# The S5 state scan of a two-block model: tables built in the feed forward before it and kept in DRAM, two groups by 64 states on the partitions, rounds overlapped

## The reference

```
for direction in (0, 1):
    bu_re = jnp.einsum('sgc,gpc->sgp', us, bb_re[direction])
    bu_im = jnp.einsum('sgc,gpc->sgp', us, bb_im[direction])
    ...
    _, _, h_re, h_im = lax.associative_scan(
        _s5_combine, (a_re, a_im, bu_re, bu_im), reverse=(direction == 1), axis=0)
    y = y + (jnp.einsum('sgp,gcp->sgc', h_re, cr[direction])
             - jnp.einsum('sgp,gcp->sgc', h_im, ci[direction]))
y = (y + d_skip.astype(f32) * u).astype(h.dtype)
z = jax.nn.gelu(y)
return (z @ w_glu_a) * jax.nn.sigmoid(z @ w_glu_b)
```

## Time and profile before

| | us |
|---|---|
| median of three runs | 3797.86 (3797.72 to 3806.94) |
| the profiled execution | 3796.62 |
| its span | 3794.7 |
| first feed forward, first matmul to last | 2379.6 to 2838.0 |
| S5, from there to the first matmul of `glu` | 2838.0 to 3209.9 |
| `glu`, second feed forward, end | 3209.9 to 3794.7 |

### The profile page before, as it was taken

How to read it: one execution, slowest core, us unless ns; L and a number is a source line. 1 busy time by engine, 2 the same in 40 slices (tenths; PEclk the granted TensorE clock), 3 DMA queues, 4 the chain that set the end, 5 groups by cost and what they waited for, 6 DMA issues and landing times. The chain is left out here.

```text
span 3794.7 us, 26215 instructions
## 1 busy us (share of the span) xinstructions
PE 3338.5 (88%) x9256; PEld 1562.0 (41%) x9256; DVE 1858.3 (49%) x3813; ACT 726.8 (19%) x1533; POOL 762.4 (20%) x680
## 2 busy tenths in 40 slices
PE   8999799888987888788788999999996777999998
PEld 3444444333433333333333454444444454444443
DVE  5556722676777777776741653115006995110000
ACT  2233211222222222222212111101003222010000
POOL 0110000344444444444420000000002442000000
PEclk9999899999999998988999999999997887999999
DMA  5643312999999999999971310222110000112221
GB/s 190 230 157 119 126 54 77 397 421 421 405 414 422 421 421 421 422 416 414 421 308 61 139 56 33 93 74 77 67 56 23 14 14 25 67 67 78 78 72 73
DMA packets 113540, 743.98 MB, mean 196 GB/s; under 512 B 13136, under 2 KB 13904, under 8 KB 30864
## 3 DMA queue, kind: packets, MB, share of 16 engines
q0 software_dynamic: 88016, 588.82, 38.2%
q1 hardware_dynamic: 25408, 153.67, 11.2%
HBM read 740.34 MB, written 2.10 MB: 196 GB/s over the span
## 5 line engine op out<-in xcount | busy, mean ns | idle before, releaser
L1283 PE MATMUL po<-pair,diag 128*128 128x512 f32 x2048 | 987.1, 640 | 226.4 <-ACT diag L1343 226.2
L1203 POOL DMA_INDIRECT pair<-in_peer_uv,idx x512 | 582.5, 1138 | 960.5 <-PE po L1283 664.1
L1430 DVE SCALAR_TENSOR_TENSOR pair<-pair,h_tm 128x1024 f32<-128x1024 f32 x512 | 617.0, 1225 | 308.1 <-DMA pair<-in_peer_uv,idx 304.4
L1283 PEld LDWEIGHTS po<-pair,diag 128*128 128x128 f32 x2048 | 409.3, 204 | 783.4 <-issue 486.2
L1574 PE MATMUL acc<-a,ring 128*128 128x512 f32 x1024 | 442.9, 593 | 0.0
L1559 PE MATMUL acc<-hT,ring 128*128 128x512 f32 x960 | 412.3, 592 | 0.0
L1574 PEld LDWEIGHTS acc<-a,ring 128*128 128x128 f32 x1024 | 195.1, 191 | 246.1 <-issue 246.1
L1559 PEld LDWEIGHTS acc<-hT,ring 128*128 128x128 f32 x960 | 182.4, 190 | 229.6 <-issue 229.6
L1599 DVE TENSOR_TENSOR a<-a 128x512 f32<-128x512 f32 x64 | 44.4, 693 | 395.0 <-ACT a L1585 395.0
L1606 DVE SCALAR_TENSOR_TENSOR xT<-acc,mod,xT 128x512 f32<-128x512 f32 x16 | 11.9, 750 | 386.9 <-PE acc L1574 386.9
L1337 ACT ACTIVATE ge<-a 128x4 f32<-128x4 f32 x128 | 26.3, 205 | 906.0 <-DVE pair L1430 905.9
(11 more groups left out here) (411 smaller groups left out, 3584.9 us busy)
## 6 DMA issues: line engine op xcount, KB each, us to landing
ring<-in_w_fc SPq DMA_DIRECT2D x62, 1024.0 KB, 4.8
mg<-in_ada_w POOLq DMA_DIRECT2D x96, 512.0 KB, 5.1
ring<-in_w SPq DMA_DIRECT2D x15, 1024.0 KB, 4.8
first<-in_w_first SPq DMA_DIRECT2D x14, 1024.0 KB, 5.7
other<-in_w_first SPq DMA_DIRECT2D x14, 1024.0 KB, 4.9
pair<-in_peer_uv,idx POOLq DMA_INDIRECT x512, 14.8
ring<-in_w_glu SPq DMA_DIRECT2D x7, 1024.0 KB, 4.8
first<-in_w_peer SPq DMA_DIRECT2D x4, 1024.0 KB, 5.4
```

The costliest lines, as they stand in the source:

```text
L1203: pool.indirect_dma_start(out=pair[:, at, :], out_offset=None, in_=core.dram["peer_uv"][:, :], in_offset=bass.IndirectOffsetOnAxis(ap=idx[ ...
L1283: last = pe.matmul(po[:, t % 2, half * 512:(half + 1) * 512], diag[:, at, :], pair[:, at, D + half * 512:D + (half + 1) * 512], start=firs ...
L1430: dve.scalar_tensor_tensor(row, row, 1.0, h_tm[:, t, :], ALU.mult, ALU.mult, accum_out=a[:, g, s:s + 1]).then_inc(dotted, 1)
```

## The change

`s5_tables` takes the place of `s5_powers` as `beside`. It makes the powers in a layout with two groups by 64 states on the partitions (real and imaginary parts now lie side by side in a row, so no swap products exist), and then all round-dependent tables: input weights `tp`, output weights `w2`, cosines, signed sines `turn`, and `decay`. They are 128 x 3328 floats a round (1.7 MB), 16 rounds. VectorE and ScalarE make them between the tiles of the feed forward, GpSimd's queue writes them to DRAM. The stage `s5` replaces the three old stages. SP reads the tables back, four rounds buffered. TensorE works on round i+1's weights while VectorE scans round i, and takes the outputs of round i-1. Products of 64-row halves write different PSUM banks. The rounds are unrolled. The order of the second block's state parameters in DRAM changes with the layout. Core of the diff (`...` marks what is left out):

```diff
         block = st.block()
         if beside:
-            block.gpsimd(load)
+            block.gpsimd(pool)
+        powers_at, rounds_at = [0, 1, 2, 4, 7], [9, 12, 15, 18, 21, 24, 27, 30]
         @block.sync
...
                 act.activation(a[:, n, :], acc[:, n % 3, :], ACT.Relu).then_inc(taken, 1)
+                if beside and n in powers_at:
+                    scalar_powers(act, powers_at.index(n))
+                if beside and n in rounds_at:
+                    scalar_round(act, rounds_at.index(n))
             if beside:
-                scalar(act)
-            act.preload_act_table_set(LN_EXP)
+                scalar_round(act, 8)
             for j in range(KT):
+                if j == KT - 1:
+                    act.preload_act_table_set(LN_EXP)
                 act.wait_ge(added, j + 1)
                 sums.square(act, j)
+                if beside and j < KT - 1:
+                    scalar_round(act, 9 + j)
             sums.root(act)
         @block.vector
...
                 dve.tensor_tensor(a[:, n, :], a[:, n, :], a[:, n, :], ALU.mult).then_inc(squared, 1)
+                if beside and n == 0:
+                    vector_powers(dve)
+                if beside and n in rounds_at:
+                    vector_round(dve, rounds_at.index(n))
             if beside:
-                vector(dve)
+                vector_round(dve, 8)
             for j in range(KT):
                 dve.wait_ge(half_made, 2 * j + 2)
                 x = core.xT[:, j, :]
                 at = gate_col(2 * layer + 1) + j
                 dve.scalar_tensor_tensor(x, acc[:, (N1 + j) % 3, :], core.mod[:, at:at + 1], x, ALU.mult, ALU.add).then_inc(added, 1)
+                if beside and j < KT - 1:
+                    vector_round(dve, 9 + j)
...
+        for r in range(ROUNDS):
+            eng.wait_ge(prepared, r + 1)
+            eng.wait_ge(sined, r + 1)
+            eng.dma_start(core.scratch[r * P:(r + 1) * P, :], table[:, r % 2, :]).then_inc(written[r % 2], 16)
+            if r + 2 < ROUNDS:
+                eng.dma_start(bc[:, r % 2, :], block_of(core, "s5_bc", r + 2)).then_inc(bc_landed[r % 2], 16)
+        for sem in written:
+            eng.wait_ge(sem, 8 * ROUNDS)
...
+    def scalar_round(act, r):
+        if r == 0:
+            act.wait_ge(ready, 5)
+        if r >= 2:
+            act.wait_ge(written[r % 2], 16 * (r // 2))
+        act.wait_ge(tabled, r + 1)
+        turn = piece(r, "turn").rearrange("p (d i q n) -> p d i q n", d=2, i=2, q=2)
+        cos = piece(r, "ct").rearrange("p (g n) -> p g n", n=SN)
+        flat = ang[:, :, :].rearrange("p (d q) n -> p d q n", d=2)
+        act.activation(turn[:, :, 1, :, :], flat, ACT.Sin)
+        act.activation(turn[:, :, 0, :, :], flat, ACT.Sin, scale=-1.0)
+        act.activation(cos, ang[:, :, :], ACT.Abs).then_inc(a_step, 1)
+        act.wait_ge(a_step, r + 1)
+        act.activation(cos, cos, ACT.Sin, scale=-1.0, bias=quarter[:, 0:1]).then_inc(sined, 1)
+    step_of = []
...
+    def vector_round(dve, r):
+        step = step_of[0]
+        here = slice(4 * r, 4 * r + 4)
+        if r >= 1:
+            dve.wait_ge(sined, r)
+        if r >= 2:
+            dve.wait_ge(written[r % 2], 16 * (r // 2))
+        step(dve.tensor_tensor(ang[:, :, :], no[:, :, :], th8[:, here].unsqueeze(2).to_broadcast([P, 4, SN]), ALU.mult))
+        reduced(dve, step, ang[:, :, :], turns[:, :, :], exact=False)
+        dve.tensor_scalar(ang[:, :, :], ang[:, :, :], PI_SAFE, -PI_SAFE, ALU.min, ALU.max).then_inc(tabled, 1)
+        decay = piece(r, "decay").rearrange("p (d i q n) -> p d i q n", d=2, i=2, q=2)
+        rate = r8[:, here].rearrange("p (d q) -> p d q", d=2).unsqueeze(3).to_broadcast([P, 2, 2, SN])
+        for i in range(2):
+            step.mark(dve.tensor_tensor(decay[:, :, i, :, :], keep[:, :, i, :, :], rate, ALU.mult))
+        dve.wait_ge(bc_landed[r % 2], 16 * (r // 2 + 1))
+        b = bc[:, r % 2, 0:128].rearrange("p (i g c) -> p i g c", i=2, g=4)
+        cc = bc[:, r % 2, 128:384].rearrange("p (i g c) -> p i g c", i=2, g=4)[:, :, :, 0:SC]
+        for name, power, with_, first, second in (("tp", pb, b, ALU.add, ALU.subtract), ("w2", pc, cc, ALU.subtract, ALU.add)):
+            out = piece(r, name).rearrange("p (i g t c) -> p i g t c", i=2, g=4, t=ST)
+            for n, (x, i) in enumerate(((0, 0), (1, 1), (1, 0), (0, 1))):
+                step.mark(dve.tensor_tensor(part[:, n, :, :, :], power[:, x, here, :].unsqueeze(3).to_broadcast([P, 4, ST, SC]),
+                                            with_[:, i, :, :].unsqueeze(2).to_broadcast([P, 4, ST, SC]), ALU.mult))
+            step.wait()
+            step.mark(dve.tensor_tensor(out[:, 0, :, :, :], part[:, 0, :, :, :], part[:, 1, :, :, :], first))
+            step(dve.tensor_tensor(out[:, 1, :, :, :], part[:, 2, :, :, :], part[:, 3, :, :, :], second))
+        dve.sem_inc(prepared, 1)
...
+        def _(sp):
+            for i in range(ROUNDS):
+                if i >= 4:
+                    sp.wait_ge(y_done, i - 3)
+                sp.dma_start(tab[:, i % 4, 0:N_TABLE], core.scratch[i * P:(i + 1) * P, :]).then_inc(landed[i % 4], 16)
+                sp.dma_start(tab[:, i % 4, N_TABLE:], block_of(core, "s5_bc", i)[:, 128:384]).then_inc(landed[i % 4], 16)
+                if i == 1:
...
+            def turn(i):
+                pe.wait_ge(landed[i % 4], 32 * (i // 4 + 1))
+                for ri in range(2):
+                    if i >= 1:
+                        pe.wait_ge(w1_copied, 2 * i - 1 + ri)
+                    for g in range(4):
+                        last = pe.transpose(bank[:, ri, g * P:(g + 1) * P], tp(i)[:, ri, g, :], ident[:, :])
+                    last.then_inc(turned, 1)
+            def own(i):
+                if i >= 1:
+                    pe.wait_ge(taps_copied, 2 * i)
+                for d in range(2):
+                    for ri in range(2):
+                        for q in range(2):
+                            for par in range(2):
+                                at = 2 * SP * par // 2 + 32 * q
+                                last = pe.matmul(bank[at:at + 32, 2 + par, d * (ST - 1) * SC:d * (ST - 1) * SC + P],
+                                                 c32(i, half[par])[:, ri, 2 * d + q, :], tp(i, half[par])[:, ri, 2 * d + q, :],
+                                                 start=(d == 0 and ri == 0), stop=(d == 1 and ri == 1), skip_group_check=True)
+                last.then_inc(tapped, 1)
+            def toeplitz(i, part):
+                pe.wait_ge(taps_copied, 2 * i + 2)
+                if part or i:
+                    pe.wait_ge(dm_copied, 2 * i + part)
+                for t in range(4 * part, 4 * part + 4):
+                    at = (ST - 1 - t) * SC
+                    last = pe.transpose(bank[:, 4, (t % 4) * P:(t % 4 + 1) * P], taps[:, i % 2, at:at + P], ident[:, :])
+                last.then_inc(d_made, 1)
+            def ends(i):
+                pe.wait_ge(w1_copied, 2 * i + 2)
+                if i:
+                    pe.wait_ge(framed, i)
+                for q in range(2):
+                    for d in range(2):
+                        for ri in range(2):
+                            at = ((d * 2 + ri) * 2 + q) * SN
+                            for par in range(2):
+                                last = pe.matmul(bank[half[par], 5, at:at + SN], w1[:, i % 2, ri, 2 * d + q, half[par]],
+                                                 u[:, 2 * i + q, half[par]], start=True, stop=True, skip_group_check=True)
+                last.then_inc(ended, 1)
+            def outputs(i):
+                pe.wait_ge(dm_copied, 2 * i + 2)
+                if i:
+                    pe.wait_ge(z_done, 2 * i)
+                for q in range(2):
+                    for par in range(2):
+                        pe.matmul(bank[half[par], 6 + par, q * P:(q + 1) * P], u[:, 2 * i + q, half[par]], dm[:, i % 3, 2 * par + q, :],
+                                  start=(q == 0), stop=False, skip_group_check=True)
+                pe.wait_ge(h_ready, 2 * i + 2)
+                for d in range(2):
+                    for ri in range(2):
+                        for q in range(2):
+                            for par in range(2):
+                                last = pe.matmul(bank[half[par], 6 + par, q * P:(q + 1) * P], hs[half[par], i % 2, d, ri, q, d:d + SN],
+                                                 w2(i, half[par])[:, ri, 2 * d + q, :], start=False, stop=(d == 1 and ri == 1),
+                                                 skip_group_check=True)
+                last.then_inc(y_done, 1)
...
+                    last = pe.transpose(bank[:, 4 + n % 2, g * P:(g + 1) * P], h2[:, 4 * n + g, :], ident[:, :])
+                last.then_inc(u_made, 1)
+            pe.wait_ge(u_copied, 8)
+            toeplitz(0, 0)
+            toeplitz(0, 1)
+            for i in range(ROUNDS):
+                ends(i)
+                if i + 1 < ROUNDS:
```

(40 more changed lines are left out.)

579 lines of the change are left out of this document (211 added, 368 removed).

## The result

The changed kernel takes 3584.89 us (median of four, 3582.02 to 3588.12) against 3798.39 beside it: a ratio of 0.9434, with a 95% interval of 0.9423 to 0.9445. The profiled execution took 3582.96 us.

What follows compares the result with a forecast made beforehand. The prediction took VectorE to set the pace, with table work and a contention in its chain. Feed forward 7.0 us, rounds 148 to 154 and edges the rest summed to -178.5, giving 3619 us; range 3590 to 3700.

Steps and rivals of the forecast that it cites:

- first feed forward: Stage before S5: TensorE's 6.97 us stall for its square goes and the new table work is covered; -7.0 us.
- chunks: Start of S5, from its first instruction to the rounds: taken as 36 us, bounds 25 and 49.
- 15 rounds: TensorE's row in S5 at 10.1 us a round, less the first round's missing outputs (2.8): 148.7 us.
- tail to `glu`: Serial end of S5 after the rounds, from the last ends through outputs, addition and GELU to the way back: 14.0 us.
- `glu` on: From `glu` to the kernel's end, which the change does not touch: no gain in the sum.
- wait for taps: In each round TensorE waits for the taps' copies before their transposes: 1.25 us with two copies, 0.90 before.
- outputs, full height: In each round, 8 full-height output instructions on TensorE at 109 ns: 0.9 us.
- outputs, halves: In each round, 32 half-height output instructions on TensorE: 1.9 us, or 3.5 without overlap.
- changes of shape: In each round, six or seven switches of TensorE's tile shape at about 0.1 us: 0.6 us.
- Rival 1: In the rounds, array halves don't overlap: `own` and half of `outputs` cost 3.5 us each; +51, 3670 us; chance 0.18.
- Rival 2: TensorE's clock stays at 1.2 GHz in all rounds (+134, 3753 us) or half of them (3685); chance 0.17.
- Rival 3: In the rounds, no overlap and half clock together: 24.9 us a round, +237, 3856 us, slower than before; chance 0.03.
- Rival 4: A wait taken as covered isn't (late Relu, reads or `z_done`): one to two us a round, 3635 to 3660; chance 0.10.

Runs made afterwards that it cites:

- run with the three terms as priced: Changed kernel with `own` in row pairs, `ends` and the full-height outputs one column half after the other: 3599.83 us, ratio to before 0.9477.

## Why the prediction was right in its mechanism and wrong in its size

Sign and mechanism held, and the time lies below the range. Against the forecast of the profiled execution, 3796.6 - 178.5 = 3618.1, the misses are:

| step | priced | measured | miss, us |
|---|---|---|---|
| first feed forward | -7.0 | -7.3 | -0.3 |
| chunks | 36 | 32.4 | -3.6 |
| 15 rounds | 148.7 | 114.3 | -34.4 |
| tail to `glu` | 14.0 | 19.1 | +5.1 |
| `glu` on | 0 | -1.8 | -1.8 |

**The first feed forward: right.** The stall before tile 1 went, and nothing took its place: ScalarE still waits for TensorE (149.3 us in 32 waits, 198.7 before), so no Relu was late enough to matter. The page's DMA issues stay within the 8 us allowed for a table:

```profile
s_tables<-table POOLq DMA_DIRECT2D x16, 1664.0 KB, 6.5
tab<-s_tables SPq DMA_DIRECT2D x16, 1664.0 KB, 6.4
```

**The chunks: right within their bounds.** The wait for the table is as forecast (7.75 us from its issue at 2832.38 to TensorE's load at 2840.13, where 7 were priced), and the steps behind it were a little shorter.

**The round's terms: this step failed.** In us, from the load row; the short gaps between the terms stand together as changes of shape:

| term | priced | measured |
|---|---|---|
| `ends` | 1.9 | 1.01 |
| `turn` | 0.86 | 0.86 |
| `own` | 1.9 | 0.81 |
| wait for taps | 1.25 | 1.14 |
| `toeplitz` | 0.86 | 0.84 |
| outputs, full height | 0.9 | 0.42 |
| outputs, halves | 1.9 | 1.72 |
| changes of shape | 0.6 | 0.91 |

`ends`, `own` and the full-height outputs are 2.46 us cheaper than priced, 36.9 us in 15 rounds. That is the whole miss of the rounds; the changes of shape, dearer than priced, take 4.7 us back. What failed in each is the number of pieces of the array that work side by side. I allowed overlap only where successive products lie in opposite row halves, because the one row that I had for it (60 ns) was such a stream. By the single starts above, the 60 ns put on `own` are about the price of two pieces at 128 columns, and it has four: 109/4 = 27. The 60 ns put on `ends` are about the price of one piece at 64 columns, and it has two: 58/2 = 29. The 109 ns of the full-height outputs are the price of one piece, and they have two: 54. The half products of the outputs, priced as two pieces, are two, and were near: 54 ns for 60. The run with the three terms as priced brought back only half of the miss because its orders didn't confine the work to the pieces that I had counted: the overlap reaches past queued instructions of the same piece.

The bounds written down for `ends`, 35 to 116, just missed its 32. For `own` the low end of 60 was no bound at all, but the estimate itself. The lowest row for small tiles, 35 ns, stood in the earlier trace rows, and `own` should have had it as its low end. That alone would have put the range's end 12 us lower (15 times 32 times 25 ns), and the time inside.

**The taps' wait and VectorE: right.** 1.14 for 1.25. VectorE is busy for 98.3 of 120 us, 6.3 in a round against 6.4, and late by the 0.9 and 0.4 us that its two waits show.

**The tail: priced 5 us too short, in part by the clock.** The last outputs take 4.8 us to VectorE's addition where 2.2 were priced. Their half products alone take 3.28 us instead of 1.72, at half clock, after 4.3 us without work on TensorE:

```profile
2986.80:2991.60 4.80, 4.74 (x41) 4.11 (x42) 0.00 (x0) 0.00 (x0) 0.00 (x0) 0.50 0.00 0
```

I had priced them at full clock. They also start 0.9 us late, since they wait for VectorE's addition of the outputs before, which the sum left out. The way back, from the end of the GELU to `glu`, takes 4.6 us where 1.9 were priced. `ends` came out 0.8 us cheaper.

**The rivals.** Rival 1 (no overlap, 3670) fell by the 25 ns of L2195. Its condition was misread too: `par` is the innermost loop, so successive products never share a row half there. Rival 2 (half clock, 3685 to 3753) fell too: the clock is 1.00 through all rounds, with eight transposes in `turn`, eight in `toeplitz` and a wait of 1.1 us in each. What the earlier trace rows showed of 2859 and 3029 did not carry over to these rounds. Rival 3 needed both. Rival 4 (reads that come late) shows in no wait: behind the first table no engine waits for `tab`.

**What bounded the old kernel: half right.** VectorE's row was as full as read, and the contention was there, but taking it away alone brought 7 us, in one time.

**Open.** How many instructions a piece lets wait is read from the starts and was not tested alone. Why the way back in the tail takes 4.6 us was not tried either.

## What to carry to other kernels

Price a stream of small products by the time between two starts in one piece of the array, divided by the number of pieces that its neighbours use, rows and columns alike, and give every such term the lowest row of the trace as its low end. When you write one, change the piece after at most four instructions. Before you blame a contention for a stage's length, follow the ring through the other engine as well: cutting the contention out showed that it cost almost nothing by itself. Where an overlapped loop has one wait left, look for independent work that can stand in it; here two such reorderings brought another 25 us.

## What the runs showed of the hardware

- In one piece of the array the next float32 matmul starts 109 ns after the last with 128 columns and 58 ns after it with 64. Different pieces start some 7 ns apart, whether they differ in rows and columns or in columns only. Per instruction that gives 25 ns in four alternating 64x32 pieces and 32 in two alternating column halves (64 columns).
- Four instructions in a row to one piece lose almost nothing (27 against 25 ns in `own`), eight do (68 there, 44 against 32 in `ends`), 16 cost 55 in `ends`. The next piece starts when three of the block still wait, by the single starts of five orders.
- A change of shape shows as a wait of 0.16 to 0.20 us in the load row, or as none (behind the 128x64 loads of `ends`, whether 128x128 loads follow or, in the run with `own` first, 64x32 ones).
- The granted clock was 1.00 through rounds in which 16 of 120 instructions are transposes and 1.1 us of 7.7 are a wait. After 4.3 us without work it was 0.50 for the next 4.8 us.
- A product of VectorE on two SBUF inputs took 2835 ns beside GpSimd's products and 683 without them.
